# Mixing stage of an encoder step: three operands turned by VectorE from quarter reloads instead of by TensorE

## The reference, cut to what matters

```python
h = rms_norm(x, g_mix)
z = h @ w_in                                   # 1024 -> 2048
a_in, a_gate, u, v = jnp.split(z, [512, 1024, 1536], axis=-1)
a = a_in * jax.nn.sigmoid(a_gate)              # then causal depthwise conv, width 31, over the rows
a_out = silu(layer_norm(conv(a) + conv_b, ln_g, ln_b))
v = layer_norm(v, ln_v_g, ln_v_b)
b_out = u * (tril(w_s) @ v + b_s)              # inside chunks of 128 rows, 4 heads
x = x + concatenate([a_out, b_out], -1) @ w_out
```

## Time and profile before

| | |
|---|---|
| time, median of 3 runs | 2452.66 us (2451.31 to 2457.74) |
| the profiled execution | 2455.3 us, span 2453.6 us |
| TensorE busy | 2385.9 us, 97% |
| VectorE busy | 1015.2 us, 41% |
| ScalarE, GpSimd busy | 448.8, 560.1 us |
| mean DMA rate | 174 GB/s |

### The profile page before, as it was taken

How to read it: one execution, slowest core, us unless ns; L and a number is a source line. 1 busy time by engine, 2 the same in 40 slices (tenths; PEclk the granted TensorE clock), 3 DMA queues, 4 the chain that set the end, 5 groups by cost and what they waited for, 6 DMA issues and landing times.

```text
span 2453.6 us, 33018 instructions
## 1 busy us (share of the span) xinstructions
PE 2385.9 (97%) x10639; PEld 1161.2 (47%) x10640; DVE 1015.2 (41%) x2549; ACT 448.8 (18%) x1012; POOL 560.1 (23%) x711
## 2 busy tenths in 40 slices
PE   8999999999999997999999998999999999999998
PEld 4444444444444474444444443444444444444443
DVE  1585665666678112255555543222222222222222
ACT  2222212212211122111111111111111111111111
POOL 1122232132133000011111113232323322323231
PEclk9999999999999999999999999999999999999999
DMA  6202111111132436464444327967497749797994
GB/s 238 108 30 67 39 41 58 39 53 47 40 126 106 149 127 223 148 191 124 122 130 127 117 86 271 340 220 270 169 366 264 261 165 368 262 353 270 350 353 149
DMA packets 186898, 427.31 MB, mean 174 GB/s; under 512 B 27874, under 2 KB 51962, under 8 KB 186666
## 3 DMA queue, kind: packets, MB, share of 16 engines
q1 hardware_dynamic: 155810, 351.41, 42.0%
q0 software_dynamic: 30656, 74.14, 8.3%
q10 hardware_dynamic: 336, 0.54, 0.1%
HBM read 351.89 MB, written 88.52 MB: 179 GB/s over the span
## 4 chain that ended last, share of the span: by engine, by line
PE 57%; DMA 1%; DVE 1%; issue 0%; POOL 0%; ACT 0%; POOLq 0%; SPq 0%; DVEq 0%; ACTq 0%
PE r_pss L2206 17%; PE r_psx L2206 12%; PE r_psx L2165 10%; PE r_pss L2145 9%; PE r_psk L2206 6%; PE r_pst L2195 2%; PE r_psr L2177 1%; PE r_psr L2215 1%; PE r_pss L2215 0%; PE r_pss L2207 0%; DMA table_scratch<-r_val,r_slot 0%; PE r_pss L2251 0%; DMA r_x1n<-h_scratch,e_token 0%; PE r_psx L2207 0%; PE r_psk L2207 0%
## 5 line engine op out<-in xcount | busy, mean ns | idle before, releaser
L790 PE MATMUL a_psz<-W 128*128 128x512 f32 x1088 | 480.0, 594 | 0.1
L2206 PE MATMUL r_pss<-W,r_h2T 128*64 x1312 | 432.3, 488 | 3.3 <-issue 3.3
L2207 PE MATMUL r_pss<-W,r_h2T 128*64 128x256 f32 (+1 forms) x1312 | 432.3, 488 | 0.0
L628 DVE SCALAR_TENSOR_TENSOR yacc<-aext,pcol,yacc 128x256 f32<-128x256 f32 x928 | 370.8, 477 | 0.0
L790 PEld LDWEIGHTS a_psz<-W 128*128 128x128 f32 x1088 | 203.2, 191 | 235.5 <-issue 235.0
L2206 PEld LDWEIGHTS r_pss<-W,r_h2T 128*64 128x64 f32 x1312 | 180.1, 137 | 257.3 <-issue 215.8
L2207 PE MATMUL r_psx<-W,r_x1r 128*64 128x512 f32 x656 | 290.3, 595 | 0.0
L2206 PE MATMUL r_psx<-W,r_x1r 128*64 x656 | 290.3, 595 | 0.0
L2165 PE MATMUL r_psx<-W 128*128 128x512 f32 x544 | 237.6, 594 | 1.2 <-ACT W L1724 1.2
L2145 PE MATMUL r_pss<-W,r_h2T 128*128 128x512 f32 x512 | 225.4, 598 | 2.3 <-PEq L123 2.3
L2207 PEld LDWEIGHTS r_pss<-W,r_h2T 128*64 128x64 f32 x1312 | 180.1, 137 | 0.0
(11 more groups left out here) (358 smaller groups left out, 2618.8 us busy)
## 6 DMA issues: line engine op xcount, KB each, us to landing
W<-in_w_expert_gate SPq DMA_DIRECT2D x32, 2048.0 KB, 12.1
W<-in_w_expert_up SPq DMA_DIRECT2D x32, 2048.0 KB, 11.0
W<-in_w_expert_down SPq DMA_DIRECT2D x32, 2048.0 KB, 10.3
W<-in_x_prompt SPq DMA_DIRECT2D x32, 512.0 KB, 4.2
x_scratch<-W SPq DMA_DIRECT2D x18, 512.0 KB, 3.0
r_x1r<-x_scratch SPq DMA_DIRECT2D x17, 512.0 KB, 4.4
x_scratch<-r_x SPq DMA_DIRECT2D x17, 512.0 KB, 5.2
h_scratch<-r_h SPq DMA_DIRECT2D x17, 512.0 KB, 2.6
```

Source lines behind the costliest of these rows:

```text
L628: ins = dve.scalar_tensor_tensor(out=out, in0=src, scalar=w, in1=yacc[:, i, :], op0=ALU.mult, op1=ALU.add)
L790: last = pe.matmul(psz[bank][:], hT[t.par][:, k, :], w_in[bank][:, k, :], start=(k == 0), stop=(k == KD - 1))
L2206: pe.matmul(out[0:HALF, :], xt[:, 0:HALF], W[:, bass.ds(base + at, n)], start=start, stop=stop)
L2207: return pe.matmul(out[HALF:P, :], xt[:, HALF:P], W[:, at:at + n], start=start, stop=stop)
```

## The change

x, a_tok and b_tok are no longer turned by TensorE. Each is stored to DRAM as rows (two new scratch tensors, xn_scratch and a_scratch; b uses mixb_scratch), reloaded in four quarters, and turned by one VectorE instruction. For x(s+1) SyncE's step gets `split_x` (one store, a wait for it, four loads), for a(s) `split_a` (the same), and `load_b` has four loads in place of one. VectorE's step gets the a turn ahead of the convolution's first 16 operations and the b and x turns behind the statistics of v. ScalarE no longer copies mbT or aext; instead of eight scaled copies out of PSUM in two halves it scales hT in place in eight operations (`gain_hT`) between vn and the swish. Since the turned columns now lie as p*KD + k, w_in and w_out are loaded in that order (w_out in two DMAs), the small constant rows are turned with strides, and a second g_mix copy (gm) is loaded in that order. Tile 0's x and the sample tile's a are still turned by TensorE.

```diff
+                    def split_x(t):
+                        sp.wait_ge(S["normed"], t.v + 1)
+                        need(sp, S["x_turned"], t.v - 1)
+                        settle(sp)
+                        sp.dma_start(xn_d, xn[:]).then_inc(S["xn_out"], 16)
+                        sp.wait_ge(S["xn_out"], 16 * t.v)
+                        settle(sp)
+                        load_split(sp, xs, xn_d, S["xs_here"])
...
+                    def split_a(t):
+                        sp.wait_ge(S["a_done"], t.v + 1)
+                        if t.v == 0:
+                            sp.wait_ge(S["table_sent"], 48)
+                        need(sp, S["stage_full"], t.v)
+                        settle(sp)
+                        sp.dma_start(a_d, a_tok[t.par][:]).then_inc(S["a_out"], 16)
+                        sp.wait_ge(S["a_out"], 16 * (t.v + 1))
+                        settle(sp)
+                        load_split(sp, as_, a_d, S["as_here"], DC)
...
-                        sp.dma_start(mbl[t.par].rearrange("p c n -> p (c n)"), row(mixb_d, t)).then_inc(mbl_here[t.par], 16)
+                        load_split(sp, bs, row(mixb_d, t), S["bs_here"], DC)
...
-                        sp.dma_start(w_in[bank], I["w_in"][0][:, c:c + 512].rearrange(kview, p=P)).then_inc(win_here[bank], 16)
+                        sp.dma_start(w_in[bank], I["w_in"][0][:, c:c + 512].rearrange("(p k) n -> p k n", p=P)).then_inc(win_here[bank], 16)
...
+                        if s.at(1).exists():
+                            split_x(s.at(1))
...
+                        if s.exists(PT):
+                            split_a(s)
```

On ScalarE, `evac_hT`, the mbT copy and the aext copy go, and this stands between vn and the swish:

```diff
+                    def gain_hT(t):
+                        act.wait_ge(S["x_turned"], t.v)
+                        for k in range(KD):
+                            last = act.activation(hT[t.par][:, k, :], hT[t.par][:, k, :], ACT.Copy, scale=gm[:, k:k + 1])
+                        last.then_inc(S["hT_done"], 2)
```

On VectorE (the a turn ahead of the convolution, the others behind `bn_aggr` of v):

```diff
+                        t = s.at(-1)
+                        if t.exists(PT):
+                            dve.wait_ge(S["as_here"], 16 * QUADS * (t.v + 1))
+                            need(dve, S["conv_step"], (t.half - 1) * 4 * TAPS)
+                            need(dve, S["halo"], t.half)
+                            settle(dve)
+                            turn_split(dve, aext[t.half % 2][:, :, HIST + P * t.par:HIST + P * t.par + P], as_).then_inc(S["stage_full"], 1)
...
+                        t = s.at(-3)
+                        if t.exists():
+                            dve.wait_ge(S["bs_here"], 16 * QUADS * (t.v + 1))
+                            need(dve, S["wo_psum"], 2 * (t.v - 1))
+                            settle(dve)
+                            turn_split(dve, mbl[t.par], bs).then_inc(S["b_turned"], 1)
+                        x = s.at(1)
+                        if x.exists():
+                            dve.wait_ge(S["xs_here"], 16 * QUADS * x.v)
+                            need(dve, S["u_psum"], x.v - 1)
+                            settle(dve)
+                            turn_split(dve, hT[x.par], xs).then_inc(S["x_turned"], 1)
                         if static and s.v == 0:
                             for g in range(4):
                                 memT_out(g)
```

More of the change, by code:

```diff
@@ L145, in build @@
         h3_d = nc.dram_tensor("h3_scratch", [TOK + P, D], F32, kind="Internal").ap()
+        a_d = nc.dram_tensor("a_scratch", [P, DC], F32, kind="Internal").ap()
+        xn_d = nc.dram_tensor("xn_scratch", [P, D], F32, kind="Internal").ap()
         prob_d = nc.dram_tensor("prob_scratch", [P, D], F32, kind="Internal").ap()
@@ L282, in build @@
                      "memT_done small_here sg_here sgs_zero sg_masked sgw_turned sgT_done pcol_turned pcol_done hist_turned "
-                     "hist_done hist_out table_set table_sent kv_psum kv_sbuf kv_out kt_psum kt_done").split()
+                     "gm_here xn_out xs_here hist_done hist_out table_set table_sent kv_psum kv_sbuf kv_out kt_psum kt_done").split()
             S = {n: sem("a_" + n) for n in names}
-            mbl_here = [sem(f"a_mbl_here{i}") for i in range(2)]
             x1_in = [sem(f"a_x1_in{i}") for i in range(2)]
@@ L296, in load @@
                     def load(t):
-                        need(sp, S["turned"], 2 * t.v)
+                        if isinstance(t.v, int) and t.v <= 1:
+                            need(sp, S["turned"], 2 * t.v)
+                        else:
+                            sp.wait_ge(S["xn_out"], 16 * (t.v - 1))
                         settle(sp)
                         load_x(sp, x_in[0][:], t).then_inc(S["x_here0"], 16)
-                    def store_b(t):
-                        sp.wait_ge(S["mb_done"], t.v + 1)
-                        sp.dma_start(row(mixb_d, t), mbT[:].rearrange("p c n -> p (c n)")).then_inc(S["mb_out"], 16)
+                    def split_x(t):
[6 more added lines that the diff above has]
+                        load_split(sp, xs, xn_d, S["xs_here"])
+                    def store_b(t):
+                        sp.wait_ge(S["b_done"], t.v + 1)
+                        sp.dma_start(row(mixb_d, t), b_tok[:]).then_inc(S["mb_out"], 16)
+                    def split_a(t):
[8 more added lines that the diff above has]
+                        load_split(sp, as_, a_d, S["as_here"], DC)
                     def load_b(t):
@@ L372, in step @@
                             sp.wait_ge(S["table_sent"], 48)
-                            sp.dma_start(w_out, I["w_out"][0].rearrange(kview, p=P)).then_inc(wout_here, 16)
+                            for half in range(2):
+                                sp.dma_start(w_out[:, CG * half:CG * half + CG, :],
+                                             I["w_out"][0][DC * half:DC * half + DC, :].rearrange("(p k) n -> p k n", p=P)).then_inc(wout_here, 16)
                         if s.at(-3).exists():
                             load_b(s.at(-3))
+                        if s.at(1).exists():
+                            split_x(s.at(1))
                         if s.v == 5:
@@ L760, in _ @@
                 def _(pe):
-                    def turn_x(t, half):
-                        pe.wait_ge(S["normed"], t.v + 1)
-                        need(pe, S["hT_done"], 2 * t.v + half)
-                        for j in range(4):
-                            k = 4 * half + j
-                            last = pe.transpose(pst[:, j, :], xn[:, P * k:P * k + P], ident[:])
-                        last.then_inc(S["turned"], 1)
                     def turn_first():
@@ L771, in turn_first @@
                         for k in range(KD):
-                            last = pe.transpose((pst if k < 4 else psy)[:, k % 4, :], xn[:, P * k:P * k + P], ident[:])
+                            last = pe.transpose((pst if k < 4 else psy)[:, k % 4, :], xn[:].rearrange("p (j k) -> p k j", k=KD)[:, k, :], ident[:])
                             if k % 4 == 3:
@@ L899, in step @@
                             keys_values(2 * (s.v - NT))
-                        t = s.at(-1)
-                        if t.exists():
-                            pe.wait_ge(S["b_done"], t.v + 1)
-                            pe.wait_ge(S["stage_full"], t.v + 1)
-                            for c in range(CG):
-                                last = pe.transpose(psx[:, c, :], b_tok[:, P * c:P * c + P], ident[:])
-                            last.then_inc(S["bT_psum"], 1)
-                        if s.at(1).exists():
-                            turn_x(s.at(1), 1)
                         if s.v == 0:
```

77 lines of the change are left out of this document (29 added, 48 removed).

## The result

The changed kernel takes 2516.85 us (median of 4 runs, 2513.95 to 2518.57). The kernel before took 2451.98 (4 runs, 2450.96 to 2457.74) in the same comparison. The ratio is 1.0258, with a 95% interval of 1.024 to 1.0277: slower by 2.6%. The prediction said slower, by 30 us, with a range that ended at 2500; the change costs about 65 us.

A forecast was written before the change was run, and what follows sets the result against it. TensorE sets the pace, with ScalarE's swish chain level behind it and lengthened by the change. Terms 12.6 + 2.6 + 1.5 + 11.0 + 4.2 - 1.4 - 0.2 = +30.3 gave 2483 us; range 2457 to 2500.

The forecast's parts named there:

- What bounds the kernel: TensorE sets the pace, but ScalarE's swish chain is level with it; T is when a step's gate projection starts.
- TensorE stays the bound: Rival: chain hidden, swish done by T + 29.3 before the output projection; -18 us, 2435; chance 0.10.
- The odd step: Odd steps 5 to 15: output projection at T + 33.6 instead of 31.77, +1.83 us each, TensorE idle 4.3.
- rival of a shorter chain: VectorE and ScalarE chain: narrow turns 0.6 us, eight scalings 1.6; total +16.4, 2469; chance 0.22.
- The even step: Even steps: output projection at T + 31.5 against 31.53, cost 0; TensorE's 2.2 us saved become waiting.
- The clock: TensorE's lower clock after idle gaps: 1.4 us for half of six odd gaps, even ones 0; +4.2 (0 to 8.4).
- The range: Whole kernel: 2457 (cheap turns, no slow clock, start at lower bound) to 2500 (all gaps slow-clocked, slow scalings).
- Steps 2 to 4: VectorE's backlog makes step 5 start later, +2.6 us, plus about one slow-clock hit, +1.5.
- The start: Step 1 waits for tile 1's store, reload and x turn; starts about 57.5 instead of 44.59; together +12.6 (8 to 16).
- SyncE in the steady steps: 13 more DMA issues per step, with x and other loads landing in time: cost 0.
- Step 16 and the rest: Step 16 has no x turn or scaling, -1.4 us; last steps -0.2; later stages 0.

The follow-up runs named there:

- e2: Changed kernel with the swish moved ahead of normed v in ScalarE's program order, nothing else changed: 2446.08 us, ratio 0.9962 to the kernel before.
- e4: Changed kernel with only the eight scalings moved behind the swish, normed v still first: 2457.58 us, ratio 1.0009 to the kernel before.
- e1: Changed kernel with extra unread matmuls on TensorE filling most of its wait before the output projection: 2493.0 us, ratio 1.0151 to the kernel before.
- e3: Changed kernel with tile 1's x turned by TensorE in step 0 as before, without its store and reload: 2499.73 us, ratio 1.0177.
- e6: Kernel before the change with only the swish moved ahead of normed v: 2453.41 us against 2455.55, ratio 0.9995.
- e5: Changed kernel with the swish ahead of normed v and tile 1's x turned by TensorE in step 0: 2429.55 us, ratio 0.9898.
- e7: Changed kernel with the swish ahead of normed v and x of tiles 1 to 4 turned by TensorE: 2427.5 us, ratio 0.989.
- e10: As e7, with VectorE's convolution chain stopped after tap 23 in its step 2 until GpSimd's sigmoid operation is done: 2426.2 us, ratio 0.9881.

## Why the prediction was right or wrong

**What bounds the kernel, and the direction: right.** The reading that nothing is gained by 16 turns fewer, because ScalarE's chain arrives level with TensorE, was confirmed: the wait for maT in each of the eleven steps, about 4 us odd and 2 us even, is the one that was named (4.64 and 2.60). e2 takes the chain away and every step from 5 to 15 falls to 42.97 us, which is the rival "TensorE stays the bound". Its condition, the swish done by T + 29.3, was right. What it named as the way there was not enough: "the eight scalings would have to cost nothing or run beside the swish" is e4, and there normed v still holds the swish in the odd steps, with the output projection at T + 30.9 and the time that of the kernel before. By the prediction's own numbers too, normed v's follower starts at 29.65 there. Its price of 2435 was too low as well (e2: 2446): it let steps 2 to 4 gain 1.74 us each and took the start at 12.6.

**The odd step: mechanism right, 0.45 us short.** Output projection predicted at T + 33.6, measured T + 34.05 (238.47 - 204.42). The eight scalings took 2.44 us and held the swish up for 2.35 (234.59 to 236.94) where 2.05 was estimated from copies out of PSUM. The narrow turns take 1.10 us, not 0.98. The x turn takes 2.0 us, as estimated. The rival of a shorter chain (narrow turns of 0.6, scalings of 1.6) is refuted by the same rows. By the Trainium skill's 16-byte lines (SBUF — State Buffer, Door 1: The DMA port swizzle), with a penalty for each access that crosses to a new one, the narrow turn keeps the wide one's price per element; with 2.15 ns against 1.95 the trace agrees with that reading. The same passage of the Trainium skill also calls a stride of up to 4 fp32 free, which could be read as a cheaper narrow turn; no run here shows one. The Trainium skill's one element per cycle for the transposer (Vector Engine (DVE) Microarchitecture Reference, 3.8 The reshape front-end) is not met by either row.

**The even step: predicted 0, measured +0.5 before any clock.** T + 31.5 became T + 32.0. The same two prices. Without the clock the eleven steps would have come to +17.2 (e1: 2.4 in an odd step, 0.55 in an even one) where 11.0 was predicted.

**The clock: the step that failed.** I took 1.4 us for each odd gap, counted half of the six, and nothing for the even gaps: +4.2. The odd output projections take 16.25 to 16.87 us, and all six are slow: against e1 an odd step loses 2.4 to 3.0 us to the clock, 16.3 in six. The even ones take 1.7 us more behind three of five gaps (steps 6, 10 and 14: 47.54 against 45.85), 5.3 against e1 in all. That is 21.5 us for the term of 4.2; with step 4's own and scatter it is the 23.9 us of e1. My price came from one wait of 3.34 us behind which the clock read 0.62 for 3 us. The error was to take this one recovery as the price of any gap, and to let half of the odd ones and all of the even ones pass free, for which the prediction has no reason: the row showed that a gap of 3.34 us costs 1.4, and the odd gaps that I forecast were longer. All gaps at 1.4 each, with slow scalings, gave the upper end of 2500; the price needed a bound as much as the number of gaps.

**The range.** Its ends do not follow from the terms. The cheap turns and scalings with no slow clock and a start of 8 give 2462, not 2457. All gaps at 1.4 with slow scalings give 2502, and with the start's own upper bound of 16 2506, not 2500. The measured time lies above all of these.

**Steps 2 to 4: +4.1 predicted with the clock, +6.3 measured.** Steps 2 and 3 came out at 60.76 us for the 60.2 predicted. Step 4 lasts 51.94 for 45.50. TensorE waits 3.48 us for the scalings of tile 4, its gate projection then takes 9.97 instead of 7.03, and its output projection waits another 4.10 with 5.37 for the first eight matmuls. Of the 4.10 us, 1.28 is a load of ScalarE's function table (ACT_TABLE_LOAD at 186.01) between the scalings and the swish. The kernel before has it too (at 164.76); the prediction's times for step 4 do not.

```profile
152.48 9.97 PE L821 MATMUL a_psz<-W 128*128 128x512 f32 x16 [3.48 <-ACT W L559]
...
188.92 5.37 PE L973 MATMUL a_psz<-W,a_maT 128*128 128x512 f32 x8 [4.10 <-issue]
```

**The start: +12.6 predicted, +15.7 measured.** Step 1 starts at 60.63, not 57.5. The chain is the predicted one, each part somewhat later: store issued 40.34 (not 38.2), quarter loads issued 49.85 (47.4), x turn at 54.21 (52.0), as SyncE and VectorE show:

```profile
40.34 1.09 SPq L312 DMA_DIRECT2D xn_scratch<-W  x1
...
49.85 1.78 SPq L219 DMA_DIRECT2D W<-xn_scratch  x4
```

```profile
54.21 2.01 DVE L224 STREAM_TRANSPOSE W<-W 128x1024 f32<-128x1024 f32 x1 [17.12 <-DMA W<-xn_scratch]
```

The 2.1 us at the store were there before the chain began: the place in SyncE's queue that I read from the earlier trace rows had moved. The second x load is issued at 11.35 instead of 10.43, and the two w_in loads behind it take 3.57 us to issue instead of 2.15. The store is issued between 39.3 and 40.4 in four kernels with the new setup, so the new order of its loads, which I had put at under 1 us, costs 1 to 2; which load of it was not tried. The last 0.9 us lie in the turns behind the x turn: their four groups follow each other by 0.88 us, at the lower clock, instead of 0.43. e3 shows that the start is a loss by itself.

**SyncE in the steady steps: cost 0, right.** VectorE waits for quarters only at the start (17.1 us for x) and once for the gated rows (4.8 us); in no steady step.

**Step 16 and the rest.** Step 16: -1.4 predicted, -1.2 measured. Behind it +2.8 us instead of -0.2: the stretch is 1729.8 us instead of 1727.0. Part of it is the change: steps 17 to 20 take 127.7 us instead of 126.4, and they take 127.4 to 129.1 in every kernel with the change and 126.5 in e6, which lacks it. What lies behind step 20 scatters from 1599 to 1603 us, so the other 1.5 us can't be told from chance.

**The sum.** Start 15.7, steps 2 to 4 6.3, odd steps 6 x 5.1 = 30.7, even steps 8.0, step 16 -1.2, rest 2.8: 62.3, the difference of the spans. The prediction's terms in the same order were 12.6, 4.1, 15.2, 0, -1.4 and -0.2. Of the 32 us between, 23.5 lie in the eleven steady steps: 17.3 are the clock (21.5 for 4.2) and 6.2 the longer chain (17.2 for 11.0). With the clock's term right the forecast would have been 2500. It would still have been 17 us short, by the chain, the start, steps 2 to 4 and the rest.

## What to carry to other kernels

Before work is moved off the engine that is the bound, read what its next wait is for, and follow that operation's engine in the order of its queue: here the swish was held by two blocks that it does not read, which cost nothing before (e6) and 71 us after (e2). Moving independent work to the front of an in-order engine is a free repair; do it together with the change, not after it. And an idle stretch on TensorE is priced as the wait plus the slow work behind it, here 2.4 to 3.0 us behind 4.65 us and 1.7 or nothing behind 2.6, each time it comes; take a range for it, not the price of one row. If the stretch can't be removed, a few matmuls that nobody reads take the second part away (e1).

## What the runs showed of the hardware

**A gap's second price does not follow from its length alone.** Behind 1.52 us (e4, six steps) the next eight output matmuls took 3.70 us. Behind 2.60 us they took 3.70 or 5.40, and which of them went by turns: steps 6, 10 and 14 were slow, steps 8 and 12 not; in e3 step 8 was slow too (47.5 us). Behind 4.65 us all six were slow, 6.12 to 6.74. But behind one and the same wait of 3.48 or 3.49 us ahead of step 4 the gate projection took 7.13 us in e4, 8.69 in e3, 8.83 in e1 and 9.97 to 10.01 in the changed kernel, e2 and e5, where it takes 7.03 without a wait; and the 3.34 us of the earlier trace rows cost 1.4. In the changed kernel and in e3 the even gap was free just when the odd output projection before it had been among the slowest (6.70 us and more for the first eight). Why an equal gap costs so differently was not tried and stays open.

**GpSimd is kept out by a whole chain of VectorE's operations, not by a single one.** The 128x512 operation takes 0.62 us where no such chain runs beside it, and took 9.32 us in the changed kernel, 6.79 in e7 and 5.23 before; in each it ended some 0.5 us after VectorE's chain of two-input operations, and stopping the chain ended it (e10). In the changed kernel:

```profile
128.33 9.32 POOL L508 TENSOR_SCALAR a_sig<-a_sig 128x512 f32<-128x512 f32 x1 [11.16 <-ACT a_sig L577]
```

```profile
136.29 0.88 DVE L648 SCALAR_TENSOR_TENSOR ybuf<-aext,pcol,yacc 128x256 f32<-128x256 f32 x2
```

The Trainium skill (SBUF — State Buffer, SBUF: two separate sides) has the port pair that VectorE and GpSimd share as an exclusive lock that is held for one instruction, and names VectorE's operations with two SBUF inputs among those that take it, against a GpSimd operation that reads SBUF, as this one does. The trace agrees with the kind of operation; but a lock for one instruction would let GpSimd in after some 0.4 us, and here it waited for the last of some 22 (128.33 to 137.17, at 0.4 us each).

**VectorE's 32-bit turns** of 128x512 and 128x1024 take 1.10 and 2.0 us with source steps of 4 and 8 elements, 2.15 and 1.95 ns per element; ScalarE's scaled 128x128 copies take 0.29 us each in a row out of SBUF (8 in 2.35) and 0.25 out of PSUM (4 in 1.00).

```profile
L224 DVE STREAM_TRANSPOSE W<-W 128x1024 f32<-128x1024 f32 x16 | 31.9, 1995 | 17.1 <-DMA W<-xn_scratch 17.1
L224 DVE STREAM_TRANSPOSE W<-W 128x512 f32<-128x512 f32 x17 | 18.7, 1101 | 4.8 <-DMA W<-mixb_scratch 4.8
```
